# Four local reorderings in a fused two-block transformer kernel: bias tables computed behind the FFN, half of h split inside the gate projection, w_o weight units inside the attention tail, second gated tiles evicted ahead of the rope table

## What is computed

```python
# first block, depth 1
mix = concat(mla_attention(...), silu(layer_norm(conv31(a * sigmoid(gate))))) @ w_o
h = x + rms_norm(mix, g_mix_post)
h = h + rms_norm((gelu(conv3(xn @ w_gate)) * (xn @ w_up)) @ w_down, g_ffn_post)
e = rms_norm(p @ w_ple_proj, g_ple)
h = h + sigmoid(h @ w_ple_gate) * e
# second block, two layers
x = h + (b_gate * conv3(c_gate * u)) @ w_out        # layer A: b_gate, c_gate, u = W_in rms_norm(h)
x = x + relu(rms_norm(x) @ w1)**2 @ w2
k_cmp, v_cmp, k_sel, v_sel, k_win, v_win = shared_kv(rms_norm(x, kv_norm))
x = x + nsa_attention(q, gates, ..., rel_bias) @ w_o  # layer B: 16 heads, T5 distance buckets
x = x + relu(rms_norm(x) @ w1)**2 @ w2
out = rms_norm(x, final_norm)
```

## Time and profile before

| what | value |
|---|---|
| time, median of 3 runs | 2014.56 us (2013.85 to 2014.84) |
| profiled execution, its own time | 2016.62 us |
| its span | 2014.6 us |
| PE busy | 1914.2 us, 95% of the span |
| DVE busy | 992.1 us, 49% |
| ACT busy | 763.7 us, 38% |
| POOL busy | 756.5 us, 38% |
| TensorE clock granted, mean | 0.965 of full |

### The profile page before, as it was taken

How to read it: one execution, slowest core, us unless ns; L and a number is a source line. 1 busy time by engine, 2 the same in 40 slices (tenths; PEclk the granted TensorE clock), 3 DMA queues, 4 the chain that set the end, 5 groups by cost and what they waited for, 6 DMA issues and landing times.

```text
span 2014.6 us, 25069 instructions
## 1 busy us (share of the span) xinstructions
PE 1914.2 (95%) x9252; PEld 1556.7 (77%) x9252; DVE 992.1 (49%) x1635; ACT 763.7 (38%) x1297; POOL 756.5 (38%) x319
## 2 busy tenths in 40 slices
PE   7899898999999799999999999999788899999997
PEld 6786586888888677888888888888655588888886
DVE  6656368543445644235433345631677635334444
ACT  6676544222223341233222223322288733222221
POOL 4412133534443332444554444534100035444442
PEclk9999899999999899999999999988799999999999
DMA  5202122332333233973333322333010123332321
GB/s 183 69 37 63 31 84 65 116 92 86 112 96 92 63 91 82 168 178 107 90 108 95 101 85 88 111 94 110 6 33 27 48 76 103 101 96 83 100 89 62
DMA packets 52236, 177.53 MB, mean 88 GB/s; under 512 B 5527, under 2 KB 5911, under 8 KB 52152
## 3 DMA queue, kind: packets, MB, share of 16 engines
q1 hardware_dynamic: 47952, 166.22, 26.7%
q10 hardware_dynamic: 4200, 10.15, 3.4%
HBM read 166.88 MB, written 9.47 MB: 88 GB/s over the span
## 4 chain that ended last, share of the span: by engine, by line
PE 81%; issue 9%; DVE 6%; POOL 2%; ACT 2%; DMA 0%; ACTq 0%; DVEq 0%; POOLq 0%
PE ps L401 25%; PE ps L402 25%; PE ps L403 25%; POOL WL L370 2%; PE ps L513 2%; DVE arena L2085 1%; DVE arena L2068 1%; PE ps L840 1%; PE ps L817 1%; PE ps L805 1%; ACT arena L1364 1%; DVE arena L1491 0%; PE ps L831 0%; ACT arena L1370 0%; DMA ident<-in_ident 0%
## 5 line engine op out<-in xcount | busy, mean ns | idle before, releaser
L370 POOL TENSOR_TENSOR WL<-raw,WH 128x1024 fp32r<-128x1024 f32 x295 | 736.0, 2509 | 1202.2 <-ACT WH L891 1202.1
L401 PE MATMUL ps<-XH,WH 128*128 128x512 f32 (+1 forms) x1280 | 503.1, 393 | 33.0 <-DMA ident<-in_ident 10.6
L891 ACT ACTIVATE WH<-raw 128x1024 fp32r<-128x1024 f32 x295 | 303.8, 1053 | 538.8 <-PE ps L403 481.5
L402 PE MATMUL ps<-XL,WH 128*128 128x512 f32 (+1 forms) x1280 | 500.9, 391 | 0.0
L403 PE MATMUL ps<-XH,WL 128*128 128x512 f32 (+1 forms) x1280 | 500.4, 391 | 0.0
L401 PE MATMUL ps<-HH,WH 128*128 128x512 f32 x1072 | 420.4, 392 | 3.7 <-DVE HL L1799 3.7
L402 PE MATMUL ps<-HL,WH 128*128 128x512 f32 x1072 | 419.0, 391 | 0.0
L403 PE MATMUL ps<-HH,WL 128*128 128x512 f32 x1072 | 418.8, 391 | 0.0
L401 PEld LDWEIGHTS ps<-XH,WH 128*128 128x128 f32 x1280 | 248.2, 194 | 85.4 <-issue 29.8
L403 PEld LDWEIGHTS ps<-XH,WL 128*128 128x128 f32 x1280 | 248.2, 194 | 49.1
L402 PEld LDWEIGHTS ps<-XL,WH 128*128 128x128 f32 x1280 | 248.2, 194 | 47.7
(11 more groups left out here) (236 smaller groups left out, 1730.3 us busy)
## 6 DMA issues: line engine op xcount, KB each, us to landing
raw<-in_weights SPq DMA_DIRECT2D x301, 512.0 KB, 3.6
tab<-arena ACTq DMA_DIRECT2D x1, 5120.0 KB, 78.6
arena<-tab SPq DMA_DIRECT2D x16, 256.0 KB, 3.6
ftab<-arena ACTq DMA_DIRECT2D x1, 2080.0 KB, 23.6
h<-in_xT SPq DMA_DIRECT2D x8, 256.0 KB, 8.7
out_T<-h SPq DMA_DIRECT2D x8, 256.0 KB, 2.1
arena<-ftab ACTq DMA_DIRECT2D x4, 256.0 KB
arena<-in_pT ACTq DMA_DIRECT2D x1, 512.0 KB, 3.5
```

The lines of the kernel that those rows point to most:

```text
L370: nc.gpsimd.tensor_tensor(WL[:, s, :], raw[:, s, :], WH[:, s, :].bitcast(f32), SUB)\
L401: nc.tensor.matmul(out, wh, xh, start=start, stop=False)
L402: nc.tensor.matmul(out, wh, xl, start=False, stop=False)
L891: nc.scalar.activation(WH[:, s, :], raw[:, s, :], ACT.Copy).then_inc(*m["whi"].tick())
```

## The change

Five things are edited; the arena (one big SBUF tensor cut into named areas) is laid out a little differently for the tables, with no operation added by that. The pieces of the diff stand in the order of the file: PE (`tables`, the FFN's end, layer A, `w_o2` in the attention), then ACT (the FFN, the gate projection, the attention), then DVE (start, gate projection).

```diff
-        ohs, relb, tabs, bcs = cut(12304, 1680), cut(13984, H2), cut(5636, 1680), cut(9728, GR, S)
+        ohs, relb, tabs, bcs = cut(14352, 1680), cut(16032, H2), cut(8192, 1680), cut(9728, GR, S)
...
+            def tables(part):
+                for i in part:
+                    if i == 3:
+                        pe.wait_ge(*m["tab_out"].next())
+                    w = min(S, 1680 - S * i)
+                    nc.tensor.matmul(ps[0:H2, 4 + i % 3, 0:w], relb[0:33, 0:H2], ohs[0:33, S * i:S * i + w],
                                      start=True, stop=True).then_inc(*m["tab_done"].tick())
...
             down(1, True)
+            pe.wait_ge(sems["onehot_in"], 16)
+            pe.wait_ge(sems["relb_in"], 16)
+            tables((0, 1))
             total(7, True)
             spread()
+            tables((2, 3))
...
-                if j == 1:
-                    tables()
...
+            def w_o2(part):
+                project(4, 2, 4, XH, XL, m["x_lo"], part=part)
...
+                if n == NP:
+                    pe.wait_ge(sems["l2_done"], 8 * NP)
+                    w_o2((0, 1))
                 if 1 <= n <= NP:
                     for r in range(2):
                         pair_transposes(n - 1, r)
-
-            for j in range(2):
-                project(4, 2, 4, XH, XL, m["x_lo"] if j == 0 else None)
+                if n == NP:
+                    w_o2((1, 2))
+
+            w_o2((2, 4))
             m["x_lo"].next(DC)
+            project(4, 2, 4, XH, XL)
...
                 square(c, ple[:, c, :], D)
+            act.dma_start(ohs[0:33, :], io["onehots"]).then_inc(sems["onehot_in"], 16)
+            act.dma_start(relb[0:33, :], io["relb"]).then_inc(sems["relb_in"], 16)
             upper(b.u + 3)
...
             for j in range(2):
-                upper(b.u + 3)
+                upper(b.u + 3 + j)
                 for t in range(4):
+                    if j == 1 and t == 3:
+                        upper(b.u + 5)
...
             root(D)
+            copy_table(0)
+            copy_table(1)
             for c in range(DC):
-                if c == 1:
-                    upper(b.u + 4)
                 act.wait_ge(*m["h_upd"].next())
                 nc.scalar.activation(XH[:, c, :], h[:, c, :], ACT.Copy).then_inc(*m["x_hi"].tick())
+                if c in (1, 2):
+                    copy_table(1 + c)
...
-            for j in range(3):
-                if j < 2:
...
-                if j >= 1:
-                    for t in range(4):
-                        act.wait_ge(*m["h_upd"].next())
-                        split_chunk("norm_mix_0", 4 * j - 4 + t)
+            for j in range(2):
...
+                for t in range(4):
+                    act.wait_ge(*m["h_upd"].next())
+                    split_chunk("norm_mix_0", 4 * j + t)
...
-            def pair_out(pair):
+            def pair_evict(pair):
                 act.wait_ge(sems["pv_done"], 2 * pair + 2)
                 nc.scalar.activation(O2[:, pair % 2, :], ps[:, 6, :], ACT.Copy).then_inc(sems["pv_out"], 1)
+            def pair_out(pair):
                 act.wait_ge(sems["pv_out"], pair + 1)
                 nc.scalar.activation(XH[:, pair, :], O2[:, pair % 2, :], ACT.Copy).then_inc(*m["x_hi"].tick())
...
+                if n >= 3 and n % 2 == 1:
+                    pair_evict((n - 3) // 2)
                 if 1 <= n <= NP:
                     pair_copy(n - 1, 1)
...
             prepare()
+            channels(2)
             rope_table()
-            channels(2)
             gates(2)
...
                     V.tensor_tensor(h[:, c, :], h[:, c, :], ptmp[:, t % 2, :], ADD).then_inc(*m["h_upd"].tick())
+                    if j and t:
+                        lower_chunk("norm_mix_0", c - 1)
                 close(4, 4)
                 dve.wait_ge(*m["h_upd"].upto())
+                for t in range(4) if j == 0 else (3,):
+                    lower_chunk("norm_mix_0", 4 * j + t)
```

More of the change, by code:

```diff
@@ L571, in mla_values @@
                 last.then_inc(sems["v1_done"], 1)
-            def tables():
-                pe.wait_ge(sems["onehot_in"], 16)
-                pe.wait_ge(sems["relb_in"], 16)
-                for k in range(0, 1680, S):
-                    if k >= 2 * S:
-                        pe.wait_ge(*m["tab_out"].upto(k // S - 1))
-                    w = min(S, 1680 - k)
-                    nc.tensor.matmul(ps[0:H2, 4 + k // S % 2, 0:w], relb[0:33, 0:H2], ohs[0:33, k:k + w],
+            def tables(part):
[4 more added lines that the diff above has]
+                    nc.tensor.matmul(ps[0:H2, 4 + i % 3, 0:w], relb[0:33, 0:H2], ohs[0:33, S * i:S * i + w],
                                      start=True, stop=True).then_inc(*m["tab_done"].tick())
-                m["tab_out"].next(4)
             pe.wait_ge(sems["const_ok"], 2)
@@ L1204, in split_chunk @@
                 square(c, h[:, c, :], DC, gain is None and c == DC - 1)
-            for j in range(3):
-                if j < 2:
-                    upper(b.u + 4)
-                    upper(b.u + 7)
-                    for t in range(4):
-                        act.wait_ge(*landed(4, 4, t))
-                        nc.scalar.activation(ps[:, (b.t + t) % 4, :], ps[:, (b.t + t) % 4, :], ACT.Sigmoid)\
-                          .then_inc(*m["ple_s"].tick())
-                    close(4, 4)
-                if j >= 1:
-                    for t in range(4):
-                        act.wait_ge(*m["h_upd"].next())
-                        split_chunk("norm_mix_0", 4 * j - 4 + t)
+            for j in range(2):
+                upper(b.u + 4)
+                upper(b.u + 7)
+                for t in range(4):
+                    act.wait_ge(*landed(4, 4, t))
+                    nc.scalar.activation(ps[:, (b.t + t) % 4, :], ps[:, (b.t + t) % 4, :], ACT.Sigmoid)\
+                      .then_inc(*m["ple_s"].tick())
+                close(4, 4)
+                for t in range(4):
+                    act.wait_ge(*m["h_upd"].next())
+                    split_chunk("norm_mix_0", 4 * j + t)
             upper(b.u + 4)
@@ L1801, in lower_chunk @@
                 add_square(c, gain is None and c == DC - 1)
-            for j in range(3):
-                if j < 2:
-                    for t in range(4):
-                        c = 4 * j + t
-                        dve.wait_ge(*m["ple_s"].next())
-                        dve.wait_ge(*m["h_upd"].upto(-1))
-                        V.tensor_tensor(ptmp[:, t % 2, :], bank(t), ple[:, c, :], MUL).then_inc(*m["tile_free"].tick())
-                        dve.wait_ge(*m["tile_free"].upto())
-                        V.tensor_tensor(h[:, c, :], h[:, c, :], ptmp[:, t % 2, :], ADD).then_inc(*m["h_upd"].tick())
-                    close(4, 4)
-                    dve.wait_ge(*m["h_upd"].upto())
-                if j >= 1:
-                    for t in range(4):
-                        lower_chunk("norm_mix_0", 4 * j - 4 + t)
+            for j in range(2):
+                for t in range(4):
+                    c = 4 * j + t
+                    dve.wait_ge(*m["ple_s"].next())
+                    dve.wait_ge(*m["h_upd"].upto(-1))
+                    V.tensor_tensor(ptmp[:, t % 2, :], bank(t), ple[:, c, :], MUL).then_inc(*m["tile_free"].tick())
+                    dve.wait_ge(*m["tile_free"].upto())
+                    V.tensor_tensor(h[:, c, :], h[:, c, :], ptmp[:, t % 2, :], ADD).then_inc(*m["h_upd"].tick())
+                    if j and t:
+                        lower_chunk("norm_mix_0", c - 1)
+                close(4, 4)
+                dve.wait_ge(*m["h_upd"].upto())
+                for t in range(4) if j == 0 else (3,):
+                    lower_chunk("norm_mix_0", 4 * j + t)
             V.memset(apad[:, :, 0:2], 0.0).then_inc(*m["v_ok"].tick())
@@ L1823, in _ @@
             dve.wait_ge(*m["r_ok"].upto())
-            def copy_tables():
-                for k in range(0, 1680, S):
-                    w = min(S, 1680 - k)
-                    dve.wait_ge(*m["tab_done"].next())
-                    V.tensor_copy(tabs[0:H2, k:k + w], ps[0:H2, 4 + k // S % 2, 0:w]).then_inc(*m["tab_out"].tick())
             for j in range(4):
```

10 lines of the change are left out of this document (5 added, 5 removed).

## The result

The changed kernel takes 1995.64 us, the median of 1995.64, 1995.45 and 1997.62, beside 2014.7 us for the kernel before on the same chip. The ratio is 0.9908, 95% interval 0.9889 to 0.9928. The forecast was 1993.0 with a range of 1987 to 2001.

The account below looks back on a forecast made before the run. PE, busy 95% of the span, was taken as the bound, so only its waits and lower-clock matmuls could go. Terms 1.5 - 0.5 + 0 + 4.1 + 5.3 + 7.0 + 4.2 = 21.6 us gave 1995.0, then 1993.0; range 1987 to 2001.

Parts of the forecast that it names:

- Start (+1.5): Kernel start: second gated tiles ahead of the rope table end PE's 5.4 us wait, a 4.0 us one replaces it; +1.5 us.
- Start of the FFN (-0.5): FFN start: two DMA issues on ACT move in front of a cast PE waits for; -0.5 us, bounds 0 and -0.9.
- End of the FFN (0): FFN end: moved casts delay `total` some 3.4 us, unslowed operations give 3.5 back; 0, bounds -3.5 and +3.5.
- The second rival: FFN end: POOL's subtractions cost time and nothing comes back; 3.4 us less gain, 1996.4 us, chance 0.1.
- Gate projection (+4.1): Gate projection: earlier splitting of chunks 0 to 3 brings `total` to 733.8, PE held about 1.2 us; +4.1, bounds 1.7 and 5.4.
- Tables (+5.3): Layer A: without table matmuls 7.8 us to be had, but a late unit limits PE to +5.3; bounds 4.2 and 7.8.
- The third rival: Layer A and FFN end: loads early enough (7.8 for 5.3) and sums slipped between subtractions (+3.5); 1987.0 us, chance 0.1.
- Attention, the loop (+7.0): Attention loop: bank 6 evicted ahead of the copies removes six PE waits of 1.16 us; +7.0, bounds 3.2 and 7.5.
- the ring: Attention loop: PE, DVE and ACT wait on each other in turn; DVE idles 3.5 and ACT 2.2 us per 17.4 us turn.
- Attention, the tail (+4.2): Attention tail: wait falls from 2.57 to 1.3 us and two groups keep the full clock; 1.2 + 3.0 = 4.2, bounds 1.2 and 4.5.
- my first rival: Attention: tail keeps the lower clock, copies give back half in the loop; 3.0 + 3.6 less, 1999.6 us, chance 0.15.
- The last step: End of the sum: 1995.0 for a profiled execution, lowered because the runs' median lay 2.1 us below it; 1993.0.

Follow-up runs that it names:

- second execution of before: The kernel before the change, run once more with nothing edited, one execution: 2013.16 us.
- the last kernel: Changed kernel with FFN-end casts re-placed, the attention tail's last but one eviction earlier, and the FFN-start cast ahead of the squares: 1978.08 us, ratio 0.982 to before.

## Why the prediction was right, and where not

*Start (+1.5):* 1.3. The wait moved to POOL's pieces, 4.29 us where I said 4.0, for the reason given: ACT's sine and cast come later.

*Start of the FFN (-0.5):* the wait grew from 3.05 to 3.22 us, 0.2 for two issues; the other 0.5 us of that line of the table are small drifts between 97 and 305 us that no wait explains.

*End of the FFN (0):* right, and by the mechanism given: three stretched sums (1.67, 2.25, 2.24), `total` about 3 us later, chunks that run free (0.69 us for 2.83). It cost 0.5 us in the pair of traces and 0.3 put back by itself. The second rival (3.4 lost, nothing back) didn't come.

*Gate projection (+4.1):* 4.4, and with the line above 3.9; put back alone 4.75. PE is held 0.8 us where I said 1.2.

*Tables (+5.3): the step that failed.* It said that "ACT's own chain doesn't move by that", and that the store's issue, "5.07 us long", would then end at 802.4, so that a late unit takes back 2.5 of the 7.8 us. I carried the issue's length over as if it belonged to the instruction. It was 0.63 us. In the stage's own terms ACT's chain came 9.3 us earlier where I said 4.2, and PE waited for no unit. What the stage gave, 8.5 us (8.2 with the second execution of before, 8.7 when put back), is all of PE's time for the tables and the restart. That is above my upper bound of 7.8, because the restart cost 1.95 us where I had 1.4 to 1.7, and the tables 6.55 for 6.4. The third rival, which had 7.8 here, named that case; its other half, sums that slip in between the subtractions (+3.5), didn't come.

*Attention, the loop (+7.0):* 6.95. Six turns at 1.23 us are 7.4, and about 0.4 us went the other way among the short matmuls between 1435 and 1482 us. No other link of PE, DVE and ACT closed the ring.

*Attention, the tail (+4.2):* 4.2 in the profiled execution, but not in each. The step "close to the 1.16 us waits, which leave the clock alone" doesn't hold. Of nine traces with a wait of 1.33 us there, four kept the clock, three lost 3.2 to 3.3 us and two about 1.7. With the wait of 2.58 us it fell in all three. So my first rival, the tail that keeps the lower clock, is true in about half of the executions, and its other half (copies that give back) in none.

*Layer B, untouched (0): missing from the sum.* It costs 3.05 to 3.07 us, with no wait and no edit in it. The granted clock (column before the last two) in the two stretches that differ, of the changed kernel and then of the kernel before:

```profile
1359.00:1363.00 4.00, 4.00 (x11) 3.13 (x11) 1.00 (x3) 0.64 (x3) 4.00 (x2) 0.50 0.60 168
...
1408.00:1412.30 4.30, 4.30 (x22) 4.30 (x22) 0.42 (x3) 0.00 (x0) 0.00 (x0) 0.50 0.00 0
```

```profile
1371.70:1376.00 4.30, 4.30 (x16) 3.46 (x16) 1.00 (x3) 0.86 (x3) 4.30 (x3) 0.71 0.58 148
...
1421.00:1425.20 4.20, 4.20 (x27) 4.20 (x26) 0.27 (x1) 0.00 (x0) 0.00 (x0) 0.61 0.00 0
```

The matmuls run at half clock behind short ones in both kernels, and longer in the changed one. The 14 traces fall into two groups with nothing between. Eight others came to this stretch between 8.0 us ahead of the changed kernel and 1.5 behind it, and lost the 3.07 us, all within 0.1. Five came 12.95 ahead (the last kernel) or 8.4 to 12.9 behind (those with the tables in layer A, the kernel before among them), and didn't. So it is not a cost of any edit: the last kernel has the changed kernel's code there and didn't pay it. That it goes by when PE arrives is what the grouping suggests, and it isn't shown. Four of the five have the tables in layer A, so that only the last kernel tells arrival from the tables.

Each execution also brings something of its own. PE starts 10.6 to 10.8 us into the span in all 14 traces, with the same matmuls, but their starts change from 0.43 us apart to 0.23 between 13.7 and 16.3 us. Two microseconds of it, in the kernel with the split put back and then in that with the casts put back (same columns as above; 10 matmuls and 6):

```profile
14.00:16.00 2.00, 2.00 (x10) 1.61 (x10) 1.49 (x1) 2.00 (x4) 2.00 (x1) 1.00 1.07 396
```

```profile
14.00:16.00 2.00, 2.00 (x6) 1.52 (x6) 1.46 (x1) 2.00 (x4) 2.00 (x1) 1.00 1.06 391
```

The granted clock reads 1.00 in both, so here the matmuls tell more than that column. The three executions with the earliest change, at 13.7 to 13.8 us, all kept the clock at the FFN's start; of the ten others with that wait, one did. That points to something that differs from the start of an execution; it isn't shown. The Trainium skill ("TensorE: Matmul & The Clock Gate", Part 1) says that the moment at which the clock changes varies with when the first matmul arrives, and not with the kernel's own start; a first change that varies by 2.6 us behind starts 0.2 us apart agrees with that, and nothing in the account rests on it.

*The last step, from the profiled execution to the median (-2.1):* the sum gave 1995.0 for an execution like the profiled one, and that took 1995.64. I then took off 2.1 because the profiled execution of before lay that much above its median. That offset was a fall of the clock at the FFN's start (2.8 us), which not every execution of before had; it is no constant to be carried to another kernel. The changed kernel's median, 1995.64 us, is its profiled execution, 2.6 us above the forecast: 2.1 are this step and 0.6 the sum's own miss.

## What to carry to other kernels

Removing a wait is worth its length, and the matmuls at the lower clock behind it only in those executions in which the clock falls; put that second part into the range, not into the sum, and compare kernels of this kind matmul by matmul in the traces, since one such fall is worth up to 3 us and can move the median of four runs by that. A cast, and the subtraction it sets off, should stand where DVE does no sums of two SBUF operands that PE waits for; three of them, moved away from such sums, gave 3.9 us. One more, that PE waited for, gave 3.2 us ahead of the squares, and 2.8 more in the one trace of it, where the clock no longer fell behind the wait. And a duration that one trace shows for the issue of a DMA is the duration at that place, not of that instruction.

## What was not expected of the hardware

- The issue on ACT of the same store of 5 MB took 0.63 us in ten executions and 4.56 to 5.50 in the four in which the tables are made right ahead of it (and lie at another column of the arena), with 0.68 us for the issue before it in all. Pads ahead of it changed nothing. The cause stays open.
- The clock behind a wait is not given by the wait: 1.33 us was followed by 2.4 GHz in four executions and by 1.2 GHz, wholly or for a part, in five; 3.05 to 3.22 us at the FFN's start by 1.2 GHz in nine and by none of it in four, with both outcomes in two executions of the kernel before.
- In an untouched stretch that loss was one of two values 3.07 us apart, and in all 14 traces the value can be told from the time at which PE came there; that this time decides it is not shown.
